# Causal rows packed in a compact ring, index scores by head pairs, and TensorE's products and turns alternated in both attentions

## The chip, the cores and the metric

The kernel runs on one core of a Trainium2 chip. The time is that of the device, in microseconds (us), median of three executions. The engines run their own instruction streams in order and wait for each other on semaphores: TensorE (PE, matmuls and transposes into PSUM), ScalarE (ACT), VectorE (DVE), GpSimd (POOL, which works on SBUF alone), and SyncE, which starts DMAs. PSUM has eight banks of 128 x 512 floats.

## What is computed

Four layers on 1024 tokens of width 1024. Two are of the first kind and two of the second:

```python
# first kind, twice
proj = rms_norm(x, g) @ w_in                      # aq, ak, av, ag, bq, bk, bv, bg
p = softmax(q*d**-0.5 @ k.T + rel_bias)           # 4 heads x 2 maps of 64
a = p[0] - lam * p[1];  oa = rms_norm(a @ v) * silu(ag)   # "attention a"
ob = softmax(q @ k.T) @ v * silu(bg)              # "attention b": 8 heads of 64, 2 key heads
x = x + rms_norm(concat(oa, ob) @ w_out)

# second kind, twice
proj = (layer_norm(x) * (1 + scale) + shift) @ w_in
y_a = silu(z_a) * (u * (w_spatial_causal @ layer_norm(v) + b_spatial))
score = sum_h w_idx[h] * relu(q_idx[h] @ k_idx.T) # 8 index heads of 64, one key
keys = the 256 best causal scores of each query
y_b = silu(z_b) * (softmax(q @ k.T over those keys) @ val)   # "attention x", 8 heads
x = layer_norm(alpha * x + gate * (concat(y_a, y_b) @ w_out))
```

## The kernel before

Every phase is written out by hand as one program for each engine. Products of floats are done as sums of three products of parts (a high part rounded for the fast mode, and the rest as a low part), so ScalarE copies a tile out of PSUM as `_hi` and VectorE subtracts that from the tile to give `_lo`.

**heads_phase** does attention b (tag `b_`, all 1024 keys) and attention x (tag `x_`, causal: row block g sees `keys(g)` = 128 to 1024 keys, with a mask added). It counts steps g, one for each of NB = 64 blocks of 128 queries of one head. In step g:

- TensorE: `product(e)` for the tiles turned two steps earlier (probabilities times values, two matmuls a tile, L981 and L982, all into PSUM bank 7), then in odd steps `scores(g+1)` for two heads at once (12 matmuls, L1001), then `turn(e)` for this step's tiles (four 128 x 128 transposes a tile, L966, PSUM banks 4 to 6).
- VectorE: `shift(g)` (L885: scores plus mask, negated, with the row minimum), `invert(g-1)` (L893, reciprocal of the sums), and the `_lo` parts of the tiles turned in step g-1 (L872).
- ScalarE: the `_hi` parts of those tiles (L824), then, where g = 4n+13, `close(n)`: it waits until the last product of group n is done (`pv_done`) and copies the two halves of bank 7 out (L831, L834); then `exponent(g)` (L840). The stream is in order, so the exponent stands behind `close`.
- GpSimd: `prob(g-1)` times the reciprocal (L936), and in the same steps as `close` the sum and the gate of the output (L916, L921).

The plan (a table made before the loops) puts the eight tiles of group n (four row blocks of one head) in steps 4n+8 to 4n+11, two a step; so the last two products of group n are in step 4n+13. In the causal form a group in the lower half has four tiles, one a step, and one in the upper half eight. The first product of the next group waits until bank 7 was read (`o_read`). `scores(g+1)` waits for `shifted(g)`: the score banks 0 to 3 hold one pair.

Probabilities lie in a ring of RING = 16 rows of 1024. For attention x four of these rows are lent by the tile `v`, so GpSimd first adds the bias to v and multiplies it into y, a piece in each of steps 1 to 8 (`gate`, L926 and L928), and `shift(12)` waits for all of it.

**diff_phase** does attention a in the same manner: a step has one head's block with both maps, `product` (three matmuls a tile, L1305 to L1307), `scores(g)` every step (12 matmuls, L1321), `turn` (L1289, banks 4 and 5). ScalarE's `read_out(n)` (L1126, L1129) comes in steps g = 4n+11, waits for the last product of group n, and stands ahead of `exponents(g-1)` (two, L1139) and of the `_hi` parts of the next step (L1120). VectorE's order in a step is `weigh(g-2)` (waits for the exponents), `_lo` parts (L1168), `shift(g)` (two passes, L1184). Before a new head 16 transposes ("nat") are in the step.

**index_phase** first turns keys and the eight index heads, each staged twice side by side (a high and a low copy of 64 columns), in ten rounds z: staging by ScalarE and VectorE (L2352, L2354, L2392, L2395), eight transposes (L2425), and a copy out by both (L2359, L2400). Then for each of 48 units (row block, head): two or four matmuls (L2438, L2439), `relu` by ScalarE (L2367), and a multiply-add into the mask row by VectorE (L2408, L2411). ScalarE's relus have two buffers.

Of the kernel before, what the change touches and what calls it, by code (L numbers as in the profile page):

```python
# [16 lines left out]
ALU = mybir.AluOpType  # L17
# [667 lines left out]
def heads_phase(nc, env, tag, groups, queries, group_of, y_of, bias=None, load=(), ahead=(), lent=(), gating=()):  # L685
# [30 lines left out]
    def keys(g):  # L716
        return (query_tile(g) + 1) * P if causal else S

# [30 lines left out]
    with ExitStack() as c:  # L749
# [5 lines left out]
        pr = sb("prob", [P, RING - len(lent), S])  # L755
# [31 lines left out]
        def ring_row(g):  # L787
            slot = g % RING
            return pr[:, slot, :] if slot < RING - len(lent) else lent[slot - RING + len(lent)]

        def prob(g):
            return ring_row(g)[:, 0:keys(g)]

        with Phase(nc) as ph:
# [63 lines left out]
            def _(dve):  # L858
# [16 lines left out]
                def shift(g):  # L875
# [35 lines left out]
            def _(pool):  # L911
# [18 lines left out]
                for g in range(START, END + 1):  # L930
                    if 1 <= g <= NB:
                        if g <= len(gating):
                            gate(g - 1)
# [3 lines left out]
                                                ALU.mult).then_inc(normed, 1)  # L937
                    n = (g - READ) // QB
# [4 lines left out]
            def _(pe):  # L943
                def turn(e):
# [16 lines left out]
                    else:  # L961
# [3 lines left out]
                        for i in range(tile_lo(n, j) // P, QB):  # L965
                            mm = nc.tensor.transpose(ps[:, bank(e), i * P:(i + 1) * P],  # L966
                                                     ring_row(rows_in(n)[i])[:, j * P:(j + 1) * P], ident[:, :])
# [37 lines left out]
                for g in range(START, END + 1):  # L1005
                    for e in plan.get(g - 2, []):
                        product(e)
                    if g % 2 and 0 <= g + 1 < NB:
                        scores(g + 1)
                    for e in plan[g]:  # L1010
                        turn(e)

def diff_phase(nc, env, aq, ak, av, gate_tiles, neg_lam, gain, first):
# [27 lines left out]
    with ExitStack() as c:  # L1042
# [23 lines left out]
        with Phase(nc) as ph:  # L1066
# [203 lines left out]
            def _(pe):  # L1270
# [68 lines left out]
                for g in range(START, END + 3):  # L1339
                    for e in plan.get(g - 2, []):  # L1340
# [7 lines left out]
                    for e in plan.get(g, []):  # L1348
# [955 lines left out]
def index_phase(nc, env, q_idx, k_idx, q_st, masks, mask_at, early):  # L2304
# [5 lines left out]
    Z = B_HEADS + 2  # L2310
    with ExitStack() as c:
# [3 lines left out]
        room = sb("i_room", [P, 3, S])  # L2315
        stg = room[:, 0:3, :].rearrange("p z (t c) -> p z t c", c=2 * HD)
        rl = room[:, 0:2, :]
        k_st = sb("i_keys", [P, 2, S], F32R)
        wsc = sb("i_weight", [P, T, B_HEADS])
        units = [(qb, h) for qb in range(FIRST, T) for h in range(B_HEADS)]  # L2320

        def stack(z):
            return k_st[:, z, :] if z < 2 else q_st[:, z - 2, :]

        with Phase(nc) as ph:
            (stg_act, stg_dve, turned, ev_act, ev_dve, scaled, sc_done, relued, summed, cut, zeroed) = [
                ph.sem(n) for n in ("stg_act", "stg_dve", "turned", "ev_act", "ev_dve", "scaled", "sc_done",
# [213 lines left out]
```

## Time and profile before

| | |
|---|---|
| median of 3 executions | 3168.41 us (3166.29 to 3173.77) |
| the profiled execution | 3164.96 us, span 3163.2 us |
| granted TensorE clock, mean of the span | 0.928 |
| busy share | PE 86%, DVE 64%, ACT 50%, POOL 36% |

Busy time by stage, read from the trace in stretches (us from the start of the span):

| stretch | stage | length | PE | DVE | ACT | POOL | clock |
|---|---|---|---|---|---|---|---|
| 355 to 573 | attention a, layer 1 | 218 | 172.20 | 149.36 | 133.16 | 141.06 | 0.87 |
| 573 to 776 | attention b, layer 1 | 203 | 183.30 | 167.62 | 164.45 | 110.62 | 0.95 |
| 1899.5 to 1967.7 | index, layer 3 | 68.2 | 54.00 | 56.41 | 46.88 | 3.96 | 0.93 |
| 2175 to 2325 | attention x, layer 3 | 150 | 115.51 | 100.58 | 108.38 | 100.68 | 0.86 |

### The profile page before, as it was taken

What the parts mean: (1) busy time and instruction counts of PE and PEld (TensorE: products, weight loads), DVE (VectorE), ACT (ScalarE), POOL (GpSimd) and SP (SyncE); (2) the same over time, 40 slices, a digit from 0 to 9 for tenths busy, and PEclk for the clock granted to TensorE, in tenths of its full rate; (3) what the DMA queues carried; (4) which work ended last, traced back from release to release, by engine and by line L of the source; (5) the groups of instructions that cost most, each with busy time, mean ns of one, the idle gap of its engine ahead of it and who ended that gap; (6) DMA issues with size and microseconds to landing.
All of it is one profiled execution on the core that took longest, in us unless ns stands there. A gap on an engine that the chain in (4) does not pass through costs nothing. (4 is left out here: it accounts for less than half of the span.)

```text
span 3163.2 us, 41488 instructions
## 1 busy us (share of the span) xinstructions
PE 2716.8 (86%) x13952; PEld 2125.2 (67%) x13952; DVE 2025.3 (64%) x4346; ACT 1578.6 (50%) x3061; POOL 1146.0 (36%) x981
## 2 busy tenths in 40 slices
PE   6999788698979997987989797996889697996887
PEld 5877566476868775665767585775667575774666
DVE  4372387597434624867974348897767358897756
ACT  3221276588422113756972216674864317674861
POOL 0100277464001003764630001985631001985631
PEclk9999899899989997998999898997999899997989
DMA  4443110100324421001013100110022100110022
GB/s 122 121 137 101 77 39 7 41 1 28 119 68 133 136 73 55 20 7 41 1 62 118 54 21 24 46 46 24 1 105 82 63 22 19 47 44 24 1 87 80
DMA packets 90754, 181.96 MB, mean 58 GB/s; under 512 B 12552, under 2 KB 27912, under 8 KB 90504
## 3 DMA queue, kind: packets, MB, share of 16 engines
q1 hardware_dynamic: 74124, 150.69, 14.8%
q10 hardware_dynamic: 16416, 28.61, 3.0%
q8 instruction: 111, 1.82, 0.2%
q14 instruction: 103, 0.84, 0.1%
HBM read 149.87 MB, written 33.33 MB: 58 GB/s over the span
## 5 line engine op out<-in xcount | busy, mean ns | idle before, releaser
L681 PE MATMUL ps<-w_hi,hh 128*128 128x512 f32 (+1 forms) x640 | 241.1, 377 | 22.2 <-DVE w_lo L566 10.1
L1236 POOL TENSOR_SCALAR a_prob<-a_prob,a_ratio 128x1024 f32<-128x1024 f32 x64 | 71.9, 1124 | 506.7 <-DVE a_ratio L1195 506.7
L681 PE MATMUL ps<-w_hi,hl 128*128 128x512 f32 (+1 forms) x640 | 241.3, 377 | 0.0
L681 PE MATMUL ps<-w_lo,hh 128*128 128x512 f32 (+1 forms) x640 | 240.1, 375 | 0.0
L1658 PE MATMUL ps<-o_w_hi,hh 128*128 128x512 f32 x512 | 211.6, 413 | 32.2 <-DVE o_w_lo L1582 32.2
L2120 DVE TENSOR_SCALAR_CACHE_REDUCE select_rows<-masks,select_cuts 128x1024 bf16<-128x1024 int16 (+7 forms) x264 | 228.1, 867 | 0.2
L1658 PE MATMUL ps<-o_w_hi,hl 128*128 128x512 f32 x512 | 207.9, 406 | 0.0
L1658 PE MATMUL ps<-o_w_lo,hh 128*128 128x512 f32 x512 | 207.0, 404 | 0.0
L936 POOL TENSOR_SCALAR b_prob<-b_prob,b_recip 128x1024 f32<-128x1024 f32 x128 | 144.2, 1127 | 162.7 <-DVE b_recip L893 160.2
L1638 POOL TENSOR_TENSOR o_rstd<-o_rstd,nhalf 128x1 f32<-128x1 f32 x56 | 46.7, 833 | 422.5 <-DVE o_rstd L1519 243.2
L1184 DVE CUSTOM_DVE_ANT_0 a_prob<-ps,a_bias 128x1024 f32<-128x1024 f32 x128 | 151.6, 1221 | 58.9 <-PE ps L1321 58.9
L885 DVE CUSTOM_DVE_ANT_1 b_prob<-ps,b_zero 128x1024 f32<-128x1024 f32 x128 | 155.8, 1219 | 45.8 <-PE ps L1001 45.8
L872 DVE TENSOR_TENSOR b_attn_t_lo<-ps,b_attn_t_hi 128x512 fp32r<-128x512 f32 x256 | 163.6, 680 | 14.5 <-ACT b_attn_t_hi L824 13.7
L840 ACT ACTIVATE b_prob<-b_prob,b_neg_max 128x1024 f32<-128x1024 f32 x128 | 147.5, 1153 | 34.4 <-DVE b_neg_max L885 34.0
L1139 ACT ACTIVATE a_prob<-a_prob,a_neg_max 128x1024 f32<-128x1024 f32 x128 | 146.3, 1151 | 36.3 <-DVE a_neg_max L1184 36.3
L2289 PE MATMUL ps<-hh,w_hi 128*128 128x512 f32 x384 | 152.1, 396 | 8.1 <-ACT y L2043 5.4
L824 ACT ACTIVATE b_attn_t_hi<-ps 128x512 fp32r<-128x512 f32 x256 | 139.2, 599 | 37.5 <-PE ps L966 36.9
L681 PEld LDWEIGHTS ps<-w_hi,hh 128*128 128x128 f32 x640 | 121.7, 190 | 51.1 <-DVE w_lo L566 19.8
L1934 PE MATMUL ps<-w_hi,hh 128*128 128x512 f32 (+1 forms) x384 | 139.9, 364 | 17.6 <-DVE w_lo L1902 12.6
L1321 PE MATMUL ps<-a_rows 64*128 64x512 f32 x768 | 120.8, 452 | 39.6 <-DVE a_neg_max L1184 35.8
L1239 POOL TENSOR_TENSOR a_prob<-a_prob 128x1024 f32<-128x1024 f32 x64 | 152.6, 2385 | 5.3
L502 ACT ACTIVATE w_hi<-w_raw 128x512 fp32r<-128x512 f32 (+1 forms) x56 | 33.7, 601 | 237.6 <-PE ps L681 229.6
(363 smaller groups left out, 8047.6 us busy)
## 6 DMA issues: line engine op xcount, KB each, us to landing
w_early<-in_w_in SPq DMA_DIRECT2D x108, 256.0 KB, 2.8
ada_w<-in_w_ada ACTq DMA_DIRECT2D x96, 256.0 KB, 2.7
w_raw<-in_w_in SPq DMA_DIRECT2D x84, 256.0 KB, 2.8
xcur<-aq SPq DMA_DIRECT2D x16, 512.0 KB, 4.0
y<-xcur SPq DMA_DIRECT2D x16, 512.0 KB, 3.7
a_bias<-bias_tiles SPq DMA_DIRECT2D x8, 960.0 KB, 4.8
bq<-in_w_out SPq DMA_DIRECT2D x12, 512.0 KB, 3.5
closing_rows<-in_w_out SPq DMA_DIRECT2D x12, 512.0 KB, 4.6
```

What stands on the lines that cost most here:

```text
L681: mm = nc.tensor.matmul(o, lhs, rhs, start=(k == 0 and i == 0), stop=(k == K - 1 and i == 2))
L840: nc.scalar.activation(prob(g), prob(g), ACT.Exp, bias=nm[:, g % NS:g % NS + 1], scale=-1.0, accum_out=sums[:, g % NS:g % NS + 1]).then_in ...
L872: nc.vector.tensor_tensor(atl[:, kk % SLOTS, lo:], ps[:, bank(e), lo:], ath[:, kk % SLOTS, lo:].bitcast(F32), ALU.subtract).then_inc(tl_do ...
L885: nc.vector.tensor_tensor_reduce(out=row_view(prob(g), g), in0=score_view(g), in1=added, scale=-1.0, scalar=3.0e38, op0=ALU.add, op1=ALU.m ...
L936: nc.gpsimd.tensor_scalar(prob(b), prob(b), rr[:, b % NS:b % NS + 1], 0.5, ALU.mult, ALU.mult).then_inc(normed, 1)
L1139: nc.scalar.activation(row, row, ACT.Exp, bias=nm[:, g % NS, m:m + 1], scale=-1.0, accum_out=out).then_inc(exped, 1)
L1184: nc.vector.tensor_tensor_reduce(out=row, in0=ps[:, 2 * m:2 * m + 2, :].rearrange("p b n -> p (b n)"), in1=bias, scale=-1.0, scalar=3.0e38 ...
L1239: nc.gpsimd.tensor_tensor(row0(g), row0(g), row1(g), ALU.add).then_inc(combined, 1)
L1658: mm = nc.tensor.matmul(o, lhs, rhs, start=(k == 0 and i == 0), stop=(k == K - 1 and i == 2))
L1934: mm = nc.tensor.matmul(ps[:, b, 0:n], lhs, rhs, start=(k == 0 and i == 0), stop=(k == K - 1 and i == 2))
L2120: spare_free[z] = mark(nc.vector.tensor_scalar(spare[:, z, 0:(qb + 1) * P], values, against, None, op, ALU.add, accum_out=column(count_of, ...
L2289: mm = nc.tensor.matmul(ps[:, b, :], lhs, rhs, start=(k == 0 and i == 0), stop=(k == K - 1 and i == 2))
```

## The change

1. In both attentions TensorE's step was: all products, scores, all turns. Now it is: first product, scores, first turn, the other products, the other turns. Programs of the other engines keep their order.
2. In attention x each row of the ring has only `keys(g)` columns, and none is lent by `v`; the wait of `shift(12)` is gone, and `gate` runs in steps 18, 22, ..., 46, behind that step's multiplication.
3. The index phase turns the keys once and the queries in pairs of heads without staging (five rounds), takes high and low parts from PSUM as passes of 1024 columns, VectorE's behind ScalarE's, and makes the scores of two heads at once, three products of 64 rows each, in two PSUM groups of four banks. Relus have three buffers.

```diff
@@ heads_phase
-def heads_phase(nc, env, tag, groups, queries, group_of, y_of, bias=None, load=(), ahead=(), lent=(), gating=()):
+def heads_phase(nc, env, tag, groups, queries, group_of, y_of, bias=None, load=(), ahead=(), gating=()):
+    def ring_at(slot):
+        return sum(keys(g) for g in range(slot))
-        pr = sb("prob", [P, RING - len(lent), S])
+        pr = sb("prob", [P, ring_at(RING)])
...
-            return ring_row(g)[:, 0:keys(g)]
+            return pr[:, ring_at(g % RING):ring_at(g % RING) + keys(g)]
...
-                    elif g == RING - len(lent):
-                        dve.wait_ge(mixed, len(gating))
...
-                        if g <= len(gating):
-                            gate(g - 1)
                         b = g - 1
                         pool.wait_ge(recip, b + 1)
                         nc.gpsimd.tensor_scalar(prob(b), prob(b), rr[:, b % NS:b % NS + 1], 0.5, ALU.mult,
                                                 ALU.mult).then_inc(normed, 1)
+                    if g >= 18 and g % 4 == 2 and (g - 18) // 4 < len(gating):
+                        gate((g - 18) // 4)
...
                 for g in range(START, END + 1):
-                    for e in plan.get(g - 2, []):
+                    ready, next_tiles = plan.get(g - 2, []), plan[g]
+                    for e in ready[:1]:
                         product(e)
                     if g % 2 and 0 <= g + 1 < NB:
                         scores(g + 1)
-                    for e in plan[g]:
+                    for e in next_tiles[:1]:
+                        turn(e)
+                    for e in ready[1:]:
+                        product(e)
+                    for e in next_tiles[1:]:
                         turn(e)
@@ diff_phase
                 for g in range(START, END + 3):
-                    for e in plan.get(g - 2, []):
+                    ready, next_tiles = plan.get(g - 2, []), plan.get(g, [])
+                    for e in ready[:1]:
                         product(e)
                     if 0 <= g < NB:
                         scores(g)
...
-                    for e in plan.get(g, []):
+                    for e in next_tiles[:1]:
+                        turn(e)
+                    for e in ready[1:]:
+                        product(e)
+                    for e in next_tiles[1:]:
                         turn(e)
@@ index_phase, scalar
+                nc.scalar.activation(stg.rearrange("p t (two d) -> p t two d", two=2),
+                                     k_idx[:, :, 0:HD].unsqueeze(2).broadcast_to([P, T, 2, HD]), ACT.Copy).then_inc(staged, 1)
+                for z in range(NP + 1):
+                    act.wait_ge(turned, z + 1)
+                    nc.scalar.activation(stack(z, 0), turned_pair(z), ACT.Copy, scale=scale_of(z)).then_inc(ev_act, 1)
+                for i, (qb, h) in enumerate(rows):
...
+                    act.wait_ge(sc_done, i // 2 + 1)
+                    if i >= RL:
+                        act.wait_ge(summed, i - RL + 1)
@@ index_phase, vector
+                for z in range(NP + 1):
+                    dve.wait_ge(ev_act, z + 1)
+                    nc.vector.scalar_tensor_tensor(stack(z, 1), turned_pair(z), scale_of(z), stack(z, 0).bitcast(F32),
+                                                   ALU.mult, ALU.subtract).then_inc(ev_dve, 1)
@@ index_phase, tensor
+                    if z >= 4:
+                        pe.wait_ge(ev_dve, z - 3)
...
+                for u, (qb, p) in enumerate(units):
+                    if u >= 2:
+                        pe.wait_ge(relued, 2 * (u - 1))
...
+                        for i, (qe, ke) in enumerate([(0, 0), (0, 1), (1, 0)]):
+                            for m in range(2):
+                                half = slice(m * HD, (m + 1) * HD)
+                                mm = nc.tensor.matmul(ps[:, 4 * (u % 2) + 2 * m + k0 // BANK, 0:w],
+                                                      stack(p + 1, qe)[half, tok], stack(0, ke)[half, k0:k0 + w],
+                                                      start=(i == 0), stop=(i == 2))
```

TensorE in attention b, before: the rows of an odd step with scores; `ident` marks transposes (turns), `b_values` products.

```order
L981 MATMUL ps<-b_attn_t_hi,b_values 128x512
L982 MATMUL ps<-b_attn_t_lo,b_values 128x512
L981 MATMUL ps<-b_attn_t_hi,b_values 128x512
L982 MATMUL ps<-b_attn_t_lo,b_values 128x512
L1001 MATMUL ps<-b_key_stack,b_query_stack 128x512 x12
L966 MATMUL ps<-ident,b_prob 128x128 x8
```

The same step now:

```order
L978 MATMUL ps<-b_attn_t_hi,b_values 128x512
L979 MATMUL ps<-b_attn_t_lo,b_values 128x512
L998 MATMUL ps<-b_key_stack,b_query_stack 128x512 x12
L963 MATMUL ps<-ident,b_prob 128x128 x4
L978 MATMUL ps<-b_attn_t_hi,b_values 128x512
L979 MATMUL ps<-b_attn_t_lo,b_values 128x512
L963 MATMUL ps<-ident,b_prob 128x128 x4
```

The second product moved behind the scores and the first turn. In step 4n+13 it is the last product of group n.

GpSimd at the start of attention x, before (`v<-v,s_b` and `y<-y,v` are a gate):

```order
L926 TENSOR_TENSOR v<-v,s_b 128x4x128
L928 TENSOR_TENSOR y<-y,v 128x512
L936 TENSOR_SCALAR x_prob<-x_prob,x_recip 128x128
L926 TENSOR_TENSOR v<-v,s_b 128x4x128
L928 TENSOR_TENSOR y<-y,v 128x512
L936 TENSOR_SCALAR x_prob<-x_prob,x_recip 128x128
```

Now:

```order
L931 TENSOR_SCALAR x_prob<-x_prob,x_recip 128x128 x2
L931 TENSOR_SCALAR x_prob<-x_prob,x_recip 128x256 x2
L931 TENSOR_SCALAR x_prob<-x_prob,x_recip 128x384 x2
L931 TENSOR_SCALAR x_prob<-x_prob,x_recip 128x512 x2
L931 TENSOR_SCALAR x_prob<-x_prob,x_recip 128x640 x2
L931 TENSOR_SCALAR x_prob<-x_prob,x_recip 128x768 x2
```

The gates left the first steps; each now stands alone in every fourth step from 18 on.

## Rows read from the trace of the kernel before

**Rows 1.** timeline of TensorE (PE), attention b: start us, length us, operation, count, idle
```profile
683.89 0.40 PE L982 MATMUL ps<-b_attn_t_lo,b_values 128*128 128x512 f32 x1
...
684.27 1.65 PE L1001 MATMUL ps<-b_key_stack,b_query_stack 64*128 64x512 f32 x12
...
685.85 1.09 PE L966 MATMUL ps<-ident,b_prob 128*128 128x128 f32 x8
...
686.70 0.48 PE L981 MATMUL ps<-b_attn_t_hi,b_values 128*128 128x512 f32 x1
...
687.02 0.40 PE L982 MATMUL ps<-b_attn_t_lo,b_values 128*128 128x512 f32 x1
...
689.81 1.66 PE L1001 MATMUL ps<-b_key_stack,b_query_stack 64*128 64x512 f32 x12
```

**Rows 2.** timeline of ScalarE (ACT), the same stretch
```profile
684.33 0.59 ACT L831 ACTIVATE b_o_hi<-ps 64x512 f32<-64x512 f32 x1
...
684.95 0.60 ACT L834 ACTIVATE b_o_lo<-ps 64x512 f32<-64x512 f32 x1
...
685.44 1.14 ACT L840 ACTIVATE b_prob<-b_prob,b_neg_max 128x1024 f32<-128x1024 f32 x1
...
686.70 1.09 ACT L824 ACTIVATE b_attn_t_hi<-ps 128x512 fp32r<-128x512 f32 x2
```

**Rows 3.** timeline of VectorE (DVE), the same stretch
```profile
687.12 0.16 DVE L893 RECIPROCAL b_recip<-b_sums 128x1 f32<-128x1 f32 x1
...
687.33 1.29 DVE L872 TENSOR_TENSOR b_attn_t_lo<-ps,b_attn_t_hi 128x512 fp32r<-128x512 f32 x2
...
688.53 1.22 DVE L885 CUSTOM_DVE_ANT_1 b_prob<-ps,b_zero 128x1024 f32<-128x1024 f32 x1
```

**Rows 4.** timeline of ScalarE, attention a
```profile
508.71 0.69 ACT L1126 ACTIVATE a_o_gained<-ps,g_sub 128x512 f32<-128x512 f32 x1 [0.72 <-PE ps L1307]
...
513.00 1.07 ACT L1120 ACTIVATE a_attn_t_hi<-ps 128x512 fp32r<-128x512 f32 x2
```

**Rows 5.** timeline of VectorE, attention a
```profile
513.61 1.29 DVE L1168 TENSOR_TENSOR a_attn_t_lo<-ps,a_attn_t_hi 128x512 fp32r<-128x512 f32 x2 [0.54 <-ACT a_attn_t_hi L1120]
...
514.82 1.21 DVE L1184 CUSTOM_DVE_ANT_0 a_prob<-ps,a_bias 128x1024 f32<-128x1024 f32 x1
```

**Rows 6.** timeline of TensorE, attention a
```profile
517.63 1.65 PE L1321 MATMUL ps<-a_rows 64*128 64x512 f32 x12
```

**Rows 7.** timeline of TensorE, attention x
```profile
2202.01 1.09 PE L966 MATMUL ps<-ident,x_prob 128*128 128x128 f32 x4 [7.77 <-POOL x_prob L936]
...
2237.64 1.34 PE L1001 MATMUL ps<-x_key_stack,x_query_stack 64*128 64x384 f32 x12
```

**Rows 8.** timeline of VectorE, attention x
```profile
2191.38 0.16 DVE L893 RECIPROCAL x_recip<-x_sums 128x1 f32<-128x1 f32 x1 [0.21 <-ACT x_prob L840]
...
2240.20 0.16 DVE L893 RECIPROCAL x_recip<-x_sums 128x1 f32<-128x1 f32 x1 [0.21 <-ACT x_prob L840]
```

**Rows 9.** timeline of GpSimd (POOL), attention x
```profile
2182.97 1.26 POOL L926 TENSOR_TENSOR v<-v,s_b 128x512 f32<-128x512 f32 x1
```

**Rows 10.** the line L907: duration ns min/median/max, first and last start
```profile
L907 DVE TENSOR_TENSOR b_values<-bkv,b_values x4: 691/692/694, 581.5 to 1441.9; 128x512 fp32r<-128x512 f32 x4
...
L907 DVE TENSOR_TENSOR x_values<-kv,x_values x2: 1508/1509/1510, 2183.3 to 2891.4; 128x512 fp32r<-128x512 f32 x2
```

**Rows 11.** timeline of ScalarE, first index phase
```profile
1902.73 0.60 ACT L2359 ACTIVATE i_keys<-ps 128x512 fp32r<-128x512 f32 x1 [2.06 <-PE ps L2425]
```

**Rows 12.** timeline of VectorE, first index phase
```profile
1918.74 0.42 DVE L2408 TENSOR_SCALAR masks<-i_room,i_weight 128x384 f32<-128x384 f32 x1 [1.38 <-ACT i_room L2367]
```

**Rows 13.** the line L2411: what its engine waited for (us, times)
```profile
  ACT i_room L2367: 3.8, 11
```

**Rows 14.** TensorE in two windows: length, busy (count), granted clock, DMA
```profile
2240.00:2242.00 2.00, 0.57 (x4) 1.00 0.04 8
...
2244.00:2250.00 6.00, 5.69 (x25) 0.50 0.00 0
```

More of the change, by code:

```diff
@@ L2309, in index_phase @@
     LOW = -3.0e38
-    Z = B_HEADS + 2
+    NP = B_HEADS // 2
     with ExitStack() as c:
@@ L2313, in sb, with stack, scale_of, turned_pair @@
             return c.enter_context(nc.sbuf_tensor(unique(name), shape, dt))
-        room = sb("i_room", [P, 3, S])
-        stg = room[:, 0:3, :].rearrange("p z (t c) -> p z t c", c=2 * HD)
-        rl = room[:, 0:2, :]
+        RL = 3
+        rl = sb("i_room", [P, RL, S])
+        stg = rl[:, 0, :].rearrange("p (t c) -> p t c", c=2 * HD)
         k_st = sb("i_keys", [P, 2, S], F32R)
         wsc = sb("i_weight", [P, T, B_HEADS])
-        units = [(qb, h) for qb in range(FIRST, T) for h in range(B_HEADS)]
-        def stack(z):
-            return k_st[:, z, :] if z < 2 else q_st[:, z - 2, :]
+        units = [(qb, p) for qb in range(FIRST, T) for p in range(NP)]
+        rows = [(qb, 2 * p + m) for qb, p in units for m in range(2)]
+        def stack(z, e):
+            return k_st[:, e, :] if z == 0 else q_st[:, 2 * (z - 1) + e, :]
+        def scale_of(z):
+            return HD ** -0.5 if z else 1.0
+        def turned_pair(z):
+            return ps[:, 2 * (z % 4):2 * (z % 4) + 2, :].rearrange("p b n -> p (b n)")
         with Phase(nc) as ph:
-            (stg_act, stg_dve, turned, ev_act, ev_dve, scaled, sc_done, relued, summed, cut, zeroed) = [
-                ph.sem(n) for n in ("stg_act", "stg_dve", "turned", "ev_act", "ev_dve", "scaled", "sc_done",
-                                    "relued", "summed", "cut", "zeroed")]
+            (staged, turned, ev_act, ev_dve, scaled, sc_done, relued, summed, cut, zeroed) = [
+                ph.sem(n) for n in ("staged", "turned", "ev_act", "ev_dve", "scaled", "sc_done", "relued", "summed",
+                                    "cut", "zeroed")]
             @ph.sync
@@ L2388, in _ @@
                                         ALU.mult).then_inc(scaled, 1)
[L2389 to L2400 removed]
+                for z in range(NP + 1):
+                    dve.wait_ge(ev_act, z + 1)
+                    nc.vector.scalar_tensor_tensor(stack(z, 1), turned_pair(z), scale_of(z), stack(z, 0).bitcast(F32),
+                                                   ALU.mult, ALU.subtract).then_inc(ev_dve, 1)
                 dve.wait_ge(scaled, 1)
[L2402 removed]
+                for u, (qb, h) in enumerate(rows):
                     n = (qb + 1) * P
```

76 lines of the change are left out of this document (13 added, 63 removed).

## The prediction

> **What bounds the kernel now.** I read the busy time by stage first, then the timelines of all four engines through a few steps of each attention, since the chain of waits on the page ends in the last phase and says nothing of the stages changed here. In attention b TensorE is busy 183.30 of 203 us; the others are below it. But a step is closer than the shares tell. Take the even pair of steps that opens with the scores at 684.27 and ends with the next scores at 689.81, 5.54 us later [rows 1]. VectorE's chain through them ends at the same moment: its `_lo` pair starts at 687.33, 0.63 behind the start of ScalarE's `_hi` at 686.70, its shift at 688.53, and that shift is what the scores at 689.81 wait for (1.28 us after its start) [rows 1 to 3]. So TensorE's work and the chain exponent, `_hi`, `_lo`, shift, scores are level; whatever delays ScalarE there by more than a few tenths reaches TensorE.
>
> **Part 1: the alternation.** Between two score blocks TensorE has the same matmuls as before, only in another order, so by itself it gains nothing: no row shows TensorE waiting for a turn in these steps. What moves is when the last product of a group ends. Before, it starts at 683.89 and ends at 684.29, just ahead of the scores, and ScalarE starts `close` at 684.33 [rows 1, 2]. Now that product stands behind the scores and one turn. Scores take 1.58 (684.27 to 685.85), a turn 0.43 (half of 685.85 to 686.70), a product 0.32 from its first start to its second and 0.40 to the end [rows 1]: it ends at 684.27 + 2.73 = 687.00, and `close` starts 2.7 us later. Behind it in ScalarE's stream stand the exponent (1.11 after `close` starts) and the `_hi` copies (2.37 after) [rows 2]; VectorE's reciprocal waits for the exponent, its `_lo` pair for the `_hi`, and the shift is behind them. Carried through: `_hi` at 689.41, `_lo` at 690.04, shift at 691.24, scores at 692.52 instead of 689.81, 2.7 us late. TensorE has only two tiles of work left in that time, and the second of them waits for a bank which the late `_lo` frees; the first product of the next group also waits for `close` to empty bank 7. So the 2.7 is idle time of TensorE, and since its other steps are already full, it isn't made good.
>
> How often: the close is in step 4n+13, and score blocks still follow for n = 0 to 12. 13 times in each of two phases, 26 x 2.7 = 70 us. In the 14 pairs of steps of a phase without a close the second turn comes one product (0.55) later; its `_hi` and `_lo` follow, and of the slack there I leave 0.15 (an estimate: both chains end together in rows 1 and 3): 0.4 x 28 = 11 us.
>
> Attention a has the same pattern. Before, `read_out` starts at 508.71; now the last product is behind scores, one turn and three matmuls: 1.59 + 0.43 + 0.95 (an estimate from the same spacings) = 2.97 behind the scores, 2.9 us later. Behind it stand two exponents and the `_hi` copies at 513.00, for which VectorE waited 0.54 even before; its shift started at 514.82 [rows 4, 5]. All of these go 2.9 later; the shift's two passes end near 520.1 and the scores at 517.63 [rows 6] go to 520.1, and the next block, for which VectorE has a values pass more to do, the full 2.9. Five groups of a phase have this with scores behind (n = 0 to 4), the sixth touches the drain (2 us): 16.5, twice is 33 us. Each step also has one more change from turn to product (0.32 against 0.23 to the next start), 0.09 x 64 = 6 us.
>
> In attention x only groups of the upper half have two tiles in a step; those of the lower half keep their order. n = 2, 3, 6, 7, 10, 11 have a close with scores behind. There the scores take 1.3 (2237.64) [rows 7], the turn 0.4, a short product 0.3: about 1.9, and VectorE already waited 0.21 for ScalarE's exponent at that place [rows 8], so nothing hides it. 12 x 1.9 = 23 us. Sum of part 1: 70 + 11 + 33 + 6 + 23 = +143 us. Bounds: at the low end, 60% of the late closes are absorbed by catching up afterwards (+57); above, nothing (+143) and the clock below.
>
> **Part 2: ring and gates.** The first turn of attention x waited 7.77 us for GpSimd's multiplication [rows 7]. GpSimd had a gate of 1.26 (and a second of the same kind) ahead of every one of its first eight [rows 9], while the reciprocal needed was there at 2191.38 [rows 8], some 3 us before TensorE came. Without the gates the wait is gone, what is next is VectorE's shift, as in the steps before: -7.8 x 2. The eight gates (2.6 each) now stand behind a multiplication in every fourth step, a step away from the output's two passes of the same length; GpSimd was busy 100.68 of 150 and has the time, but a group's last multiplication can be a few tenths late: +1 x 2 (0 to 5). One VectorE pass stood beside a gate and took 1.51 instead of 0.69 [rows 10], right ahead of a shift: -0.8 x 2. The Trainium skill, SBUF — State Buffer, section SBUF: two separate sides, has the reason: a VectorE operation with two SBUF inputs and a GpSimd operation lock each other out for a whole instruction. By that rule the moved gates could also hold up VectorE in the loop; but its shifts and `_lo` passes have one input in PSUM, so by the rule they are free, and the sum stays. Were they not, 16 gates of 2.6 would put up to 40 us more on it. Part 2: -15 us (bounds -18 to 0).
>
> **Part 3: the index phase.** Keys are turned by 1902.73 as before [rows 11]. Then one ScalarE pass of 1024 columns (1.14, the exponent of that width [rows 2]) and five of VectorE, each 1.22 [rows 3]: done at 1909.97. Before, the last copy ended at 1918.74 - 1.38 = 1917.36 [rows 12]. 7.4 less 0.3 for the longer first pair. The loop is VectorE's, whose passes are the same; the third relu buffer can at most take away its waits for ScalarE, 3.8 in both phases [rows 13]. TensorE's share falls, hidden either way: a pair at 1024 keys is 12 matmuls like the scores here, 1.58 [rows 1], under two VectorE passes. 9 x 2 = -18 us (bounds -22 to -8, if the wide passes take 1.5 each).
>
> **The clock.** 143 - 15 - 18 = +110. The new idle times have one more price. After an idle stretch in attention x (0.57 busy of 2.00 us) the granted clock was 0.50 for the next 6 us, with 5.69 busy [rows 14]: 1.2 instead of 2.4 GHz costs up to 2.8 there. Shorter waits left it at 1.00. The new stalls are 2 to 3 us in some 4, much like that place. No row says how often 48 of them bring it down; I take half, at 2.0 each, +40 (0 to 134). The Trainium skill, Perfetto Trace Analysis, section Matmul Optimizations, says that the matmul engine scales its power with use, so matmuls should be issued back to back in batches. By that rule the alternation costs the clock at every stall, which is my third case.
>
> So 3164.96 + 150 = 3315 for the profiled execution; the median of the runs is 3.4 above that execution: 3318 us.
>
> **The cases.** A, as worked out, 3318: chance 0.45. B, the same stalls, but the clock holds: +110, 3278, chance 0.22; for it speaks that in b it stood at 1.00 through waits of a few tenths, against it rows 14. C, the clock falls at nearly every stall: 48 x 2.0 = 96, +206, 3374, chance 0.13; the two levels in rows 14 speak for it, that TensorE is half idle in part of the low time speaks against. D, most late closes are absorbed: +57 - 33 = +24 plus little clock, 3200, chance 0.11; for it that ScalarE is busy only 164 of 203, against it that its slack lies elsewhere in the step. E, on the other side: the read-out is not late, because the slack between exponent and `_lo` covers it; then only parts 2 and 3 count, -33, 3135, chance 0.06. It decides at the `close` that starts less than a few tenths later than now, since the two chains end together [rows 1, 3]; 2.7 is well past it. F, the gains are smaller and the delays absorbed, so that both cancel: within 0.2% of 3168, chance 0.03. A measurement of this kernel can tell about 0.2% from no change.
>
> The range for 8 in 10 leaves out E and F, most of D, and the upper end of C: 3235 to 3380. Faster 0.06, same 0.03, slower 0.91.
>
> **What would show it.** Right: in attention b ScalarE idles some 2.5 us ahead of `close`, waiting for a product, 13 times a phase; VectorE's reciprocal waits for the exponent and TensorE's scores for the shift behind it; four steps take near 13.8 us instead of 11.1 (twice 5.54); attention b grows by some 40 to 55 us a phase, a by 18 to 25, x by under 10, and the index phase shrinks by 9. The wait of 7.77 us in x is gone. Wrong: closes that start at the scores as before, or late closes without idle time on TensorE; or granted clocks unchanged in the attentions (B), or at 0.8 (C).

## The result and the profile after

| kernel | median us | executions | ratio to before (95%) |
|---|---|---|---|
| before | 3167.35 | 3163.41 to 3173.77 (4) | |
| changed | 3284.04 | 3271.56 to 3290.50 (4) | 1.0362 [1.0325, 1.0398] |

Slower by 117 us: inside the range of 3235 to 3380, 34 below the forecast of 3318, and 6 above case B (3278). The profiled execution took 3281.54 (span 3279.8), 116.6 more than that of before.

Stage by stage, from the start of a stage's first matmul to that of the next stage, in the timelines (us; these are longer than the stretches for which the busy times were read):

| stage | before | changed | difference | `ring_index` (below) |
|---|---|---|---|---|
| attention a, first | 216.08 | 234.99 | +18.9 | 216.09 |
| attention b, first | 214.32 | 252.38 | +38.1 | 214.31 |
| attention a, second | 216.61 | 232.67 | +16.1 | 216.65 |
| attention b, second | 214.31 | 257.50 | +43.2 | 214.26 |
| index, both | 139.43 | 123.16 | -16.3 | 123.13 |
| attention x, first | 169.48 | 177.48 | +8.0 | 166.62 |
| attention x, second | 170.91 | 180.50 | +9.6 | 166.56 |

The projections, the selection and the output stages differ by at most 1.2 each.

In attention b, a step that closes a group. TensorE's timeline in the changed kernel (start, duration, engine and line, what, count, idle time and its releaser); it answers to [rows 1]:
```profile
646.36 1.67 PE L998 MATMUL ps<-b_key_stack,b_query_stack 64*128 64x512 f32 x12 [0.28 <-DVE b_neg_max L882]
647.96 0.66 PE L963 MATMUL ps<-ident,b_prob 128*128 128x128 f32 x4
648.37 0.48 PE L978 MATMUL ps<-b_attn_t_hi,b_values 128*128 128x512 f32 x1
648.69 0.40 PE L979 MATMUL ps<-b_attn_t_lo,b_values 128*128 128x512 f32 x1
648.92 0.60 PE L963 MATMUL ps<-ident,b_prob 128*128 128x128 f32 x4
650.47 0.47 PE L978 MATMUL ps<-b_attn_t_hi,b_values 128*128 128x512 f32 x1 [0.95 <-ACT b_o_lo L833]
...
652.99 0.66 PE L963 MATMUL ps<-ident,b_prob 128*128 128x128 f32 x4 [0.93 <-DVE b_attn_t_lo L871]
...
654.73 1.66 PE L998 MATMUL ps<-b_key_stack,b_query_stack 64*128 64x512 f32 x12 [0.62 <-DVE b_neg_max L882]
```
ScalarE's timeline over the same time, answering to [rows 2]:
```profile
645.47 1.07 ACT L823 ACTIVATE b_attn_t_hi<-ps 128x512 fp32r<-128x512 f32 x2
649.12 0.59 ACT L830 ACTIVATE b_o_hi<-ps 64x512 f32<-64x512 f32 x1 [2.58 <-PE ps L979]
649.73 0.59 ACT L833 ACTIVATE b_o_lo<-ps 64x512 f32<-64x512 f32 x1
650.35 1.15 ACT L839 ACTIVATE b_prob<-b_prob,b_neg_max 128x1024 f32<-128x1024 f32 x1
```
And VectorE's, answering to [rows 3]:
```profile
651.62 0.16 DVE L890 RECIPROCAL b_recip<-b_sums 128x1 f32<-128x1 f32 x1 [2.33 <-ACT b_prob L839]
652.25 1.29 DVE L871 TENSOR_TENSOR b_attn_t_lo<-ps,b_attn_t_hi 128x512 fp32r<-128x512 f32 x2 [0.46 <-ACT b_attn_t_hi L823]
653.45 1.21 DVE L882 CUSTOM_DVE_ANT_1 b_prob<-ps,b_zero 128x1024 f32<-128x1024 f32 x1
```
The reader sees the predicted chain: the last product of the group starts 2.33 (648.69) behind the scores, `close` starts at 649.12 (2.76 behind them) after ScalarE has idled 2.58, and the reciprocal, `_lo` and the shift follow late. TensorE's idle time comes in three pieces, not in one: 0.95 ahead of 650.47, for `close` to read bank 7 out; 0.93 ahead of 652.99, for a late `_lo`; 0.62 for the shift. The next scores start at 654.73, 8.37 behind the last ones instead of 5.54 [rows 1].

What TensorE waited for in the first attention b, of the changed kernel (releaser, us in total, times, longest):
```profile
PE ps L998 <- DVE b_neg_max L882: 22.7, 27, 5.0
PE ps L978 <- ACT b_o_lo L833: 12.4, 13, 1.0
PE ps L963 <- DVE b_attn_t_lo L871: 9.5, 12, 0.9
PE ps L963 <- DVE b_query_stack L863: 4.2, 2, 3.0
PE ps L963 <- DVE b_key_stack L863: 3.0, 1, 3.0
```
Thirteen waits of 1.0 for bank 7 and twelve of 0.8 for a late `_lo`; before, these two were 1.0 and 0.4 us in all. The wait for the shift grew by 8.0, from this:
```profile
PE ps L1001 <- DVE b_neg_max L885: 14.7, 10, 5.7
```
At two closes of a phase VectorE's copies of the next keys and queries (L863) stand behind the late chain too, and there TensorE stops for 3.04 us in one piece.

Attention a: ScalarE's timeline in the changed kernel, answering to [rows 4]; the read-out waits 2.98 instead of 0.72 (five read-outs of a phase have scores behind them):
```profile
495.33 0.69 ACT L1128 ACTIVATE a_o_gained<-ps,g_sub 128x512 f32<-128x512 f32 x1 [2.98 <-PE ps L1309]
...
496.39 1.15 ACT L1141 ACTIVATE a_prob<-a_prob,a_neg_max 128x1024 f32<-128x1024 f32 x1
```
Attention x: TensorE's first turn of probabilities, answering to the wait of 7.77 in [rows 7]: it is gone. Beside it ScalarE at one of the six late closes of a phase (two kinds of row, two fences):
```profile
2301.27 0.86 PE L963 MATMUL ps<-ident,x_prob 128*128 128x128 f32 x4
2302.16 1.34 PE L998 MATMUL ps<-x_key_stack,x_query_stack 64*128 64x384 f32 x12
```
```profile
2328.66 0.59 ACT L830 ACTIVATE x_o_hi<-ps 64x512 f32<-64x512 f32 x1 [1.29 <-PE ps L979]
```
Index phase: VectorE's last staging passes and the loop's first, answering to [rows 12]. They end at 2026.33, 9.97 after the phase's start; before it was 16.64:
```profile
2022.84 3.49 DVE L2386 SCALAR_TENSOR_TENSOR i_queries<-ps,i_queries 128x1024 fp32r<-128x1024 f32 x3 [0.48 <-ACT i_queries L2355]
2027.81 0.42 DVE L2395 TENSOR_SCALAR masks<-i_room,i_weight 128x384 f32<-128x384 f32 x1 [1.49 <-ACT i_room L2362]
```
TensorE's granted clock (the column behind the busy time and count). Changed kernel: both attentions b, then 200 us out of the middle of each:
```profile
589.00:841.20 252.20, 190.75 (x1200) 140.18 (x1201) 173.93 (x337) 173.50 (x307) 112.87 (x96) 0.95 0.04 14
1498.30:1755.80 257.50, 195.38 (x1201) 142.78 (x1201) 174.36 (x337) 173.87 (x307) 112.78 (x96) 0.92 0.04 14
629.00:829.00 200.00, 162.15 (x1039) 119.60 (x1037) 143.46 (x282) 144.31 (x259) 97.22 (x83) 0.99 0.00 1
1538.00:1738.00 200.00, 163.19 (x1033) 119.70 (x1032) 144.00 (x282) 142.72 (x256) 96.52 (x82) 0.98 0.00 1
```
Before, the middle of the first b:
```profile
611.00:770.00 159.00, 155.34 (x1034) 119.90 (x1032) 140.47 (x280) 140.36 (x258) 96.02 (x82) 1.00 0.00 1
```
With 19% idle time where there was 2%, the clock in the middle stays at 0.98 to 0.99. Whole phases show 0.85 and 0.86 in a, 0.95 and 0.92 in b, 0.86 and 0.83 in x, against 0.88, 0.87, 0.94, 0.94, 0.87 and 0.87 in `ring_index`. The stalls hardly brought it down, as case B had it. What little there is in the middle of b stands behind the pieces of 3.04, as these stretches of the changed kernel show (a close with three pieces, then one with a single piece and what follows it):
```profile
650.00:656.00 6.00, 3.98 (x26) 2.80 (x26) 3.85 (x8) 5.90 (x11) 4.80 (x4) 1.00 0.00 0
678.00:681.00 3.00, 0.06 (x1) 0.00 (x0) 0.81 (x3) 2.95 (x6) 2.41 (x2) 0.91 0.00 0
681.00:683.50 2.50, 2.40 (x10) 2.31 (x11) 1.86 (x5) 1.55 (x3) 1.24 (x2) 0.50 0.00 0
```

### The profile page after: what moved, and what is told of

Read it like the earlier page. It is cut to its first block and busy times, and to the rows that moved or that the text cites. A ratio compares the mean times of both kernels' runs of the same rounds, so it can differ in the third digit from the quotient of the medians.

```text
span 3279.8 us, 41576 instructions
## 1 busy us (share of the span) xinstructions
PE 2712.8 (83%) x14032; PEld 2116.7 (65%) x14032; DVE 2024.2 (62%) x4318; ACT 1580.0 (48%) x3035; POOL 1146.6 (35%) x981
## 3 DMA queue, kind: packets, MB, share of 16 engines
q1 hardware_dynamic: 74124, 150.69, 14.5%
## 5 line engine op out<-in xcount | busy, mean ns | idle before, releaser
L681 PE MATMUL ps<-w_hi,hh 128*128 128x512 f32 (+1 forms) x640 | 243.3, 380 | 22.2 <-DVE w_lo L566 10.1
L963 PE MATMUL ps<-ident,b_prob 128*128 128x128 f32 x1024 | 158.1, 280 | 33.5 <-DVE b_attn_t_lo L871 19.0
L882 DVE CUSTOM_DVE_ANT_1 b_prob<-ps,b_zero 128x1024 f32<-128x1024 f32 x128 | 155.9, 1219 | 43.2 <-PE ps L998 43.1
L963 PEld LDWEIGHTS ps<-ident,b_prob 128*128 128x128 f32 x1024 | 122.6, 142 | 84.5 <-DVE b_attn_t_lo L871 44.3
L998 PE MATMUL ps<-b_key_stack,b_query_stack 64*128 64x512 f32 x768 | 114.2, 431 | 49.2 <-DVE b_neg_max L882 46.2
```

Of the source, the lines that this page charges most:

```text
L681: mm = nc.tensor.matmul(o, lhs, rhs, start=(k == 0 and i == 0), stop=(k == K - 1 and i == 2))
L882: nc.vector.tensor_tensor_reduce(out=row_view(prob(g), g), in0=score_view(g), in1=added, scale=-1.0, scalar=3.0e38, op0=ALU.add, op1=ALU.m ...
```

## The experiments

My theory: a late product holds ScalarE's in-order stream, and by it everything queued behind `close` and the read-out. The rivals: TensorE's mixing of products and turns costs by itself; parts 2 or 3 cost; the clock. Where a stage is compared in what follows, the lengths come from the timelines as in the table above. `ring_index` stands for the changed kernel with the old order in both attentions. The runs were made in several sets, in which the kernel before took 3167.35, 3166.63, 3164.00 and 3163.94, so a difference of medians between sets is good to some 3 us; each ratio is to before in the same set.

**`ring_index`: the alternation undone.**
```
-  for e in ready[:1]: product(e)
-  scores; for e in next_tiles[:1]: turn(e)
-  for e in ready[1:]: product(e)
-  for e in next_tiles[1:]: turn(e)
+  for e in plan.get(g - 2, []): product(e)
+  scores; for e in plan[g]: turn(e)
```

> The changed kernel with the alternation undone in both attentions: ring, gates and index phase stay. Late close (my theory: only the alternation costs, because a group's last product now stands behind the scores and one turn): about 3136 us. The index phase is 2 x 8.1 shorter as in the changed kernel (61.6 instead of 69.7 us), attention x 8 us shorter in each half (near 162, not 177 and 180), attention b back at 214.3 and a at 216 us. Rival, ring and gates cost too (GpSimd's moved gates hold a multiplication or VectorE up in the loop, so that part of the +8.0 and +9.6 of attention x is theirs): attention x stays at 169 us or more, and the time is 3150 or more. Rival, order in the rest matters too (scheduling of the whole shifts everything): over 3160.

Measured: 3141.09 us, ratio 0.9918 [0.9903, 0.9932]. a and b are those of before to 0.1 us, the index phases take 123.1. x takes 166.6, neither 162 nor 169, and the time is 5 above the 3136 expected: parts 2 and 3 are a gain, the whole loss is the alternation's (3284.04 - 3141.09 = 143), and part 2 gave half of what it should.

**`alt_only`: the kernel before with the alternation alone** (the same lines, added to before).

> The kernel before with the alternation alone in both attentions' loops; gates and index phase as before. Late close: attention a near 234, b 252 to 257, x near 186 (170 + 12 late closes of 1.4, a phase has six: +8 to +16 on the 170) and the index phase at 69.7; in all 3167 + 35 (a) + 81 (b) + 25 to 35 (x) = 3308 to 3318 us. Rival, ring and gates carry part of the loss in attention x: x is at or below 177 here too, and the time under 3300.

Measured: 3296.45, 1.0411 [1.0388, 1.0434]; a +15.9 and +17.9, b +43.7 and +41.4, x +11.9 and +10.4, index unchanged. The loss is there without ring and index. The time missed its range (3308 to 3318) and even lies under the 3300 that the rival named, though the profiled execution, the slowest of four, took 3307.46; but the rival's condition, x at or below 177, did not come: x is at 181, above the changed kernel and below the 186 expected.

**`last_first`: only in closing steps all products ahead of the scores.**
```
+  first = len(ready) if (g - READ) % QB == 0 else 1     # in a: if due(g, 11) is not None
-  for e in ready[:1]: product(e)
+  for e in ready[:first]: product(e)
...
+  for e in ready[first:]: product(e)
```

> The changed kernel, but in the steps that close a group (n of b and x, and the read-out's step of a) all products stand ahead of the scores; all the other steps keep the alternation. Late close: ScalarE's idle time of 2.2 to 2.6 us ahead of close goes, and with it nearly all of the loss; only what the later second turn of the other steps costs stays (in the prediction 11 us in b, 6 us of switches in a): 3136 + 10 to 17 = 3146 to 3153 us, b near 220 us, a near 220. Rival, the alternation itself costs (TensorE's changes between turns and products in every step, banks, a clock that falls): three steps of four keep it, so at least half of the loss stays, over 3210 us.

Measured: 3167.78, 1.0004 [0.9995, 1.0014]. Of the 143 us 116 are gone; 27 stay, more than the 10 to 17 (the time is 15 above its range). b is +7.8, a +5.9 and +5.8, x about +2.5 over `ring_index`. ScalarE's wait ahead of `close` in the first b is back from 35.6 (16 times) to:
```profile
ACT b_o_hi L830 <- PE ps L979: 2.2, 3, 1.6
```

**`closing_only`: the counterpart, alternation in the closing steps alone** (`first = 1` there, `len(ready)` elsewhere).

> The counterpart of last_first: alternation only in the steps that close a group, all other steps in the old order; ring, gates and index phase as in the changed kernel. Late close: what the changed kernel has over ring_index less what last_first has over it: 3141 + 116 = 3257 us (3245 to 3265), b near 249 (214.3 + 13 x 2.65), a near 230, x near 175. Rival, the loss belongs to the mixture of turns and products as such, and last_first only profited from its closing steps being clean: with one step in four mixed about a quarter of the 143 us is left, some 3177 us.

Measured: 3267.60 (3255.14 to 3272.27; the profiled execution is the shortest), 1.0326 [1.0302, 1.0350]: against the 3257 expected the profiled execution is 3255 and the median 10 above, 3 outside its range, and both are far from the rival's 3177. Against `ring_index` a is +14.1 and +10.2, b +36.2 and +36.1, x +10.7 and +10.9: 118 us by stages. The granted clocks of the six phases are those of `ring_index` (0.88 and 0.90, 0.94 and 0.94, 0.87 and 0.87 against 0.88 and 0.87, 0.94 and 0.94, 0.87 and 0.87), so these 118 are not the clock's. The start of each of VectorE's shifts in b, less that in `ring_index`, makes the steps visible (us; first b):

| shift number | changed | `closing_only` | `exp_first` |
|---|---|---|---|
| 14 | -1.5 | 0.0 | 0.4 |
| 16 | 1.2 | 2.7 | 2.0 |
| 20 | 4.2 | 5.3 | 3.7 |
| 24 | 7.2 | 8.0 | 5.5 |
| 32 | 13.6 | 14.5 | 8.6 |
| 36 | 16.5 | 17.1 | 10.3 |
| 40 | 19.5 | 19.8 | 12.1 |

In `closing_only` a late close costs 2.6 to 2.7 us in eleven of thirteen steps (one costs 3.8, one 2.2; 2.7 in the mean), and next to nothing happens between them when the other steps are in the old order. In the changed kernel a group loses some 3.0: the close and 0.3 for the later second turn.

**`exp_first`: the changed kernel, ScalarE's exponents ahead of `close` and read-out.**
```
+  if 0 <= g < NB: exponent(g)
   if (g - READ) % QB == 0 ...: close(n)
-  if 0 <= g < NB: exponent(g)
```

> The changed kernel with its alternation, but in ScalarE's stream the exponent (b, x) and the two exponents (a) of a step stand ahead of close and of the read-out. The product is as late as in the changed kernel. Late close by what is queued behind it: the exponent no longer waits for the late product, but the _hi copies still stand behind the close, so they start at 687.00 + 1.11 = 688.1 instead of 689.4 in the prediction's times: 1.4 us late, not 2.7. In b 26 x 1.3 come back, in a 10 x 2.2 (two exponents of 1.1 leave the read-out's wait), in x about 12 x 1.0: 34 + 22 + 12 = 68, so about 3216 us (3195 to 3240). Rival, TensorE itself is held (the next product waits for the bank that close empties, or the switches cost): the order in ScalarE's stream changes nothing, 3275 or more.

Measured: 3217.83, 1.0158 [1.0143, 1.0173]. TensorE's stream is the changed kernel's, instruction for instruction, and 66 of the 143 us are gone: at least these are the price of what is queued on ScalarE behind the late product, and neither TensorE's mixing nor its order as such. a is at 217.5 (all but 1.4 recovered), b at 238.3 (14 and 19 recovered; four steps lose 1.3 to 1.9 instead of 2.9). In b that is the 34 expected, in a it is 33 instead of 22. x recovered nothing (180.1, 179.9), against the 12 expected: there GpSimd's part of the close comes later still, and its multiplications behind it. TensorE's wait for them in the first x, of `exp_first`:
```profile
PE ps L963 <- POOL x_prob L931: 13.5, 6, 4.1
```
In the changed kernel it is 7.0 (5 times).

**`close_later`: the changed kernel, `close` one step later in ScalarE's stream**, behind the next step's `_hi` copies, in b and x.
```
-  n = (g - READ) // QB;  if (g - READ) % QB == 0 ...: close(n)
+  n = (g - 1 - READ) // QB;  if (g - 1 - READ) % QB == 0 ...: close(n)
```

> The changed kernel with its alternation, but in attentions b and x ScalarE's close stands one step later in its stream, behind the next step's _hi copies, so that neither exponent nor _hi waits for the late product (attention a is as in the changed kernel, +35 us). If the loss is only what is queued behind the close on ScalarE, b is at 214.3 + 5.5 = 220 us, x near 169 and the time 3141 + 35 + 12 + 5 = 3193 us. Rival, in exp_first it was the bank: the next group's first product waits for close to read bank 7 out. Close then ends at 689.0 in the prediction's times, that product stands from 687.4 and waits 1.6 us, the scores are about 1 us late: b at 214.3 + 13 x 1.0 + 5.5 = 233 us (226 to 245), 3220 us (3205 to 3240).

Measured: 3321.42, 1.0501 [1.0483, 1.0518], worse than either expectation; b 250.6 and 249.0, 2 and 8 less than in the changed kernel where by the first expectation 32 and 38 were to go, x 201.6 and 202.0, 24 and 22 more. It excludes that only ScalarE's queue matters. The rival of this run, the bank, is right, and I priced it too low. TensorE's wait for `close` in the first b, of `close_later`:
```profile
PE ps L978 <- ACT b_o_lo L833: 27.5, 15, 2.0
```
2.0 each instead of 1.0 and 27.5 in all instead of 12.4, while the wait for the shift fell from 22.7 to 17.1 and that for a late `_lo` from 9.5 to 0.7. In x the wait for the bank is 27.7 instead of 7.1 and that for GpSimd's multiplications 14.9 instead of 7.0; TensorE is also busy for 9.8 us more there, at a granted clock of 0.81 instead of 0.86. A close that is late has two prices, by the queue and by the bank; moving it in one stream only changes which is paid.

**The gates in attention x.** The same comparison of shift starts shows where `ring_index` lost what the start of x had gained: in the first x it is 9.9 us ahead of before from row 12 to row 24, then 9.2 at row 32, 6.7 at row 36 and 2.9 from row 50 on. Four kernels, all `ring_index` but for the gates' steps (in `ring_index` 18, 22, ... 46); the last leaves the gates out, so its y is not the wanted one, and it only shows a floor.
```
gates_early          if g >= 20 and g % 4 == 0 ...: gate((g - 20) // 4)
gates_early_exp_a    the same, and exponents ahead of the read-out in a
gates_skip           at = (18, 22, 26, 34, 38, 42, 50, 54);  if gating and g in at: gate(at.index(g))
gates_none           no gate at all
```

> ring_index with each of GpSimd's eight gates two steps later in its stream, in steps 20, 24, ... 48, right behind the multiplication of a group's last row and no more between the last close and the next group's rows. In ring_index attention x is 9.9 us ahead of before at row 24 and 2.9 ahead at the end; the largest piece, 3.3 us, falls where the gate of step 46 stands ahead of rows 46 and 47 and the first turn waits 3.09 us for GpSimd. If it is the place of the gates: x near 160 to 162 us instead of 166.6, the time 3131 us (3127 to 3135). Rival, a gate costs the same in any step (GpSimd holds VectorE up, or its time is simply missing): x at 166 or more and 3138 to 3144.

Measured: 3137.36 (0.9921 [0.9906, 0.9936]); x 165.4 and 166.3. Between the two expectations on the side of the rival: two steps later, the same wait came again. GpSimd's timeline there, of `gates_early`:
```profile
2268.42 1.29 POOL L925 TENSOR_TENSOR y<-y,v 128x512 f32<-128x512 f32 x1
2269.69 1.01 POOL L931 TENSOR_SCALAR x_prob<-x_prob,x_recip 128x896 f32<-128x896 f32 x1
2270.86 1.27 POOL L913 TENSOR_TENSOR x_o_lo<-x_o_lo,x_o_hi 64x512 f32<-64x512 f32 x1
2272.20 1.27 POOL L918 TENSOR_TENSOR y<-y,x_o_lo 64x512 f32<-64x512 f32 x1
2273.57 3.21 POOL L931 TENSOR_SCALAR x_prob<-x_prob,x_recip 128x896 f32<-128x896 f32 x3
```
and TensorE's at its end:
```profile
2275.82 1.94 PE L963 MATMUL ps<-ident,x_prob 128*128 128x128 f32 x8 [2.53 <-POOL x_prob L931]
```
Gate, multiplication, close and three multiplications without a gap: GpSimd still has wide rows to multiply when TensorE's score blocks go from 1024 keys to 128 and a step becomes short.

> gates_early, and in attention a ScalarE's two exponents stand ahead of its read-out. In exp_first, despite the late read-out, the later head pairs of attention a ran 0.3 to 1.5 us ahead of the kernel before. If that came from the exponents' place, a takes 214 to 215.5 us instead of 216.1, twice: 1 to 3 us under gates_early. Rival, it came with the alternation: a is at 216 or above, and the time is that of gates_early or longer.

Measured: 3138.35 (0.9925 [0.9908, 0.9941]), a 219.9 and 217.1. No gain; the rival holds.

> ring_index with GpSimd's eight gates in steps 18, 22, 26, 34, 38, 42, 50 and 54, so that none stands where attention x goes from wide rows (1024 keys) to short ones (rows 32 and 48). gates_early did not gain there: close, gate and three multiplications stood together in either order and TensorE waited 2.5 us for the last of them, twice (ring_index 2.06 and 3.09). If it is this meeting of close and gate at the change to short rows: both waits go but for a few tenths, x takes about 162 to 163 us in each half instead of 166.6, 3133 us against 3141 (3130 to 3136). Rival, the wait there is close and multiplications alone: x at 165 or more and 3137 to 3141.

Measured: 3132.55 (3125.46 to 3136.59), 0.9896 [0.9878, 0.9914]; x 163.1 and 163.0, as expected. TensorE's wait for GpSimd in the first x fell from 6.3 in `ring_index` to:
```profile
PE ps L964 <- POOL x_prob L931: 2.4, 4, 1.0
```
It is 31 us under before and the shortest of the complete versions. By the medians alone it is not clear of `ring_index`, whose interval of the ratio (0.9903 to 0.9932) touches its own; the two x stages, 3.5 and 3.6 shorter, show the gain.

> ring_index without the eight gates in either half (the selective output's bias sum and gating multiplication are left out): the floor for any placing. If only the place of the gates cost time, attention x is here no shorter than in gates_skip, by 0.5 us at most. If a gate costs wherever it stands, x is under 161 us, 1 us or more below gates_skip in each half.

Measured: 3127.82 (0.9885 [0.9870, 0.9901]); x 157.6 and 157.8. The place of the gates is 3.6 us a phase, and another 5.3 goes with them wherever I put them. (By medians it is 4.7 for both phases; the first projections and attention a, which no gate touches, took 3.0 more in the profiled execution without gates.) These 5.3 are not time in which TensorE waits: it is idle for 36 us of the first x in both kernels. They are in its busy time, for the same matmuls, at another granted clock. First x, `gates_skip` and then `gates_none`:
```profile
2167.50:2330.60 163.10, 127.26 (x809) 97.16 (x809) 110.10 (x302) 120.62 (x271) 108.53 (x112) 0.89 0.03 10
```
```profile
2169.30:2326.80 157.50, 121.60 (x808) 93.13 (x808) 109.53 (x302) 120.07 (x271) 88.49 (x96) 0.93 0.03 11
```
Why the clock is higher without gates is not shown. VectorE is not held up by them: in the first x its shifts of 1024 columns took 1212 to 1225 ns in `gates_skip` and 1214 to 1225 in `gates_none`, its `_lo` passes of 512 columns 672 to 693 and 670 to 693.

## Why the prediction held, and where not

**Right: the mechanism of part 1, and nearly its sum.** Forecast +143 without the clock. Between `ring_index` and the changed kernel the six attention phases differ by 18.9 + 16.0 + 38.1 + 43.2 + 10.9 + 13.9 = 141.0, the medians by 143. By its steps: the late close in b was to cost 2.7 and costs 2.6 to 2.7 in eleven of its thirteen places, as `closing_only` shows; the read-out in a was to cost 2.9: its five steps in the first a are 3.0, 2.6, 2.9, 3.2 and 2.9; x 11.5 a phase: 10.8 in `closing_only`. `exp_first` shows the queue on ScalarE (66 us back with TensorE's stream untouched), `close_later` the bank, `last_first` and `closing_only` that it is the last product of a group and not mixing as such, and `closing_only` that it is not the clock.

That the sum came out to 2 us is in part luck. The late closes and read-outs alone were forecast at 126 and gave 118 (b 72 for 70, a 24 for 33, x 22 for 23), the rest at 17 and gave 27 to 32 (`last_first`), and the 141 holds some clock that the 143 was to leave out.

**The bank.** The prediction named the next group's first product, which waits for bank 7, and gave it no price. It is 1.0 in each of 13 waits; `close_later` doubled it, and b gained only 2 and 8 us although exponent and `_hi` no longer stood behind the late product. In the changed kernel it comes ahead of the wait for the late shift and is part of the 2.67.

**The second turn and the change of kind** were 11 + 6 = 17; with the closing steps in order (`last_first`) 27 stay by medians and 32 by stages. In b the shifts lose 0.3 to 0.5 in most groups of four steps, as forecast (0.4), but some 1.3 already at the start of the phase; in a it is 5.9 instead of 3, and in x 2.5 that the forecast did not have. Where the 5.9 in a come from was not tried.

**Failed: the clock, the one term that made the forecast too high.** "I take half, at 2.0 each, +40", from one place in attention x [rows 14], since "the new stalls are 2 to 3 us in some 4, much like that place". The size of a stall was right, its shape was not. At eleven closes of a phase in b it comes in pieces of at most 0.95, and behind none of these did the clock fall in the middle of b; at the other two it is one piece of 3.04, and the clock fell behind three of the four of the changed kernel. The granted clock there stayed at 0.98 to 0.99.

What the clock did cost can be bounded from the trace's record of it: in the six phases TensorE was busy for 202 us at 1.2 GHz, in `ring_index` for 161, and the 41 us more, at half the pace, are 20 us at most (an estimate). Like phases of the changed kernel differ by 5.1 (b), 3.0 (x) and 2.3 (a) with busy times that differ by 4.5, 3.9 and 1.7, so it is not nothing. It is already in the 141. The rule of the Trainium skill that I quoted (Perfetto Trace Analysis, Matmul Optimizations: issue in batches, since power scales with use) would have given case C, 3374: the trace does not agree for stalls in pieces of under 1 us, which are most of them, and agrees with it only for the few of 3.04. With that term at zero the forecast is 3278, case B.

**Failed: part 2, half of its size.** Forecast -15, measured -7.2 (x, both). The start gave what it should and more (-9.9 and -10.6 against 7.8 + 0.8 for the wait and the values pass). The values pass in x, which [rows 10] have at 1509 ns, in the changed kernel (ns, min, median, max):
```profile
L904 DVE TENSOR_TENSOR x_values<-kv,x_values x2: 692/692/693, 2291.3 to 2998.6; 128x512 fp32r<-128x512 f32 x2
```
Half of the term was lost later. The step that failed is "a group's last multiplication can be a few tenths late: +1 x 2 (0 to 5)": the gates in the loop cost 7.1 and 7.4 a phase (the lead of 9.9 and 10.6 at row 12 that is 2.8 and 3.2 at the end), outside my bounds. `gates_skip` gets 3.6 of it back by place. I counted GpSimd's share of the whole stage (100.68 of 150) and not its work between the last close and the change to short rows. The rival that I set aside, gates that hold VectorE up in the loop (up to 40 us), did not come: VectorE's passes there are as long with gates as without.

**Part 3** was -18 and is -16.3: -6.7 a phase before the loop (forecast -7.1), -1.5 in the loop, where six waits for ScalarE of 2.0 in all are gone.

Together: 143 + 40 was 141 (-42), -15 was -7 (+8), -18 was -16 (+2), the remaining stages -1: 150 becomes 117.

Two sums of the prediction do not come out. Half of 48 stalls at 2.0 us each are 48, not 40; with 48 the forecast would have been 3326, further off and still inside the range. And +57 is 40% of the whole 143; if 60% of the late closes alone (126) are absorbed, 67 are left. Of the signs, b was to grow by 40 to 55 a phase and a by 18 to 25: the first b (38.1) and the second a (16.1) lie just under that.

## What to carry to other kernels

An engine's stream is in order, so before moving an instruction, look at what waits for its result on another engine and list what is queued behind that wait; the price of a move is paid there, each time it happens. Keep the last instruction of a group early: `last_first` differs from the changed kernel in one step of four and takes back four fifths of the loss. Moving the others gained nothing here either: `last_first` is still 27 us above `ring_index`. A result that is read late also keeps its bank: the two prices add up, and a second engine's stream only shifts them. For an engine that "has the time", count its work between two deadlines, not over the stage: `gates_skip` has the same work as `ring_index` and is 3.6 us a phase shorter.

## What was not expected of the hardware

In these runs TensorE's granted clock did not follow the share of idle time but the length of its single pieces. In the middle of attention b (from 40 us behind its start to 15 ahead of its end), over the changed kernel, `alt_only`, `closing_only`, `close_later` and `exp_first`, two phases each, it stood at 1.00 but for sixteen short stretches at 0.50. Each began within 1.5 us of the end of a long piece:

- at 9 of 10 idle pieces of 3.04 us (changed, `alt_only`, `closing_only`);
- at 7 of 25 pieces of 1.87 to 2.01 us (`close_later`), and none of 4 of 1.77 (`exp_first`);
- at none of some 380 pieces of under 1 us, though in the changed kernel they come three to a late close and are most of the 19% idle time.

In the place of [rows 14] the idle piece ahead of the fall is 1.46, with shorter ones around it. Why 7 of 25 like pieces bring the clock down and the others do not is open.

Where a low clock falls moves between neighbouring stages: the first projections and attention a run the same instructions in `ring_index` and in `gates_skip`, together 528.4 and 528.2 us, but the border lies 4 us apart:
```profile
40.50:352.80 312.30, 299.78 (x1345) 243.20 (x1346) 128.24 (x242) 58.45 (x107) 13.54 (x1) 0.98 0.37 114
352.80:568.90 216.10, 170.33 (x977) 121.64 (x977) 148.65 (x301) 131.16 (x230) 141.02 (x112) 0.88 0.09 29
```
```profile
41.80:350.00 308.20, 295.70 (x1344) 239.88 (x1345) 128.23 (x242) 58.48 (x107) 13.54 (x1) 0.99 0.37 116
350.00:570.00 220.00, 173.56 (x977) 123.88 (x977) 148.68 (x301) 131.29 (x230) 141.31 (x112) 0.85 0.08 28
```
So the 3.8 of `gates_early_exp_a` in the first a, too, is no cost of its edit by itself; a stage's length next to such a border is good to some 4 us.
